# Expert row gathers: GpSimd issues the V row of the running step before the U row of the next step

## The reference, cut to what matters

```
def peer_ffn(x, w_pq, sub_keys1, sub_keys2, peer_u, peer_v):
    q = (xt @ w_pq).reshape(T, PEER_HEADS, PEER_QUERY)
    s1 = einsum(q[..., :128], sub_keys1);  s2 = einsum(q[..., 128:], sub_keys2)
    v1, i1 = top_k(s1, 16);  v2, i2 = top_k(s2, 16)
    top_s, pos = top_k(all 256 sums of v1 and v2, 16)      # 8 heads x 16 = 128 experts for a token
    gate = softmax(top_s)
    u_sel = take(peer_u, idx)                               # rows of 2048 floats
    act = gelu(einsum('thkd,td->thk', u_sel, x), approximate=False) * gate
    v_sel = take(peer_v, idx)
    out = einsum('thk,thkd->td', act, v_sel)
```

## Time and profile before

| | |
|---|---|
| median of 3 runs | 3806.15 us (3805.95 to 3826.44) |
| profiled execution: its time | 3811.37 us |
| profiled execution: span | 3809.3 us |
| PE busy | 3256.0 us (85%) |
| DVE busy | 2196.4 us (58%) |
| POOL busy | 999.7 us (26%) |
| gathers (queue q0) | 547.39 MB, 35.9% of the 16 DMA engines' time |
| weights and gates (queue q1) | 474.45 MB, 32.7% |

### The profile page before, as it was taken

The page is one execution under the profiler, slowest core; times in us unless marked ns, Lnnn a source line. Parts: engine busy times, 40 slices in busy tenths (PEclk is TensorE's granted clock), DMA queues, the critical chain, the costliest instruction groups (busy, mean ns, idle before and its releaser), DMA issues.

```text
span 3809.3 us, 32121 instructions
## 1 busy us (share of the span) xinstructions
PE 3256.0 (85%) x10214; PEld 1893.5 (50%) x10214; DVE 2196.4 (58%) x3100; ACT 378.0 (10%) x653; POOL 999.7 (26%) x674
## 2 busy tenths in 40 slices
PE   7998989899875747377444999999999999999996
PEld 4443433344333323236442666666666666666663
DVE  5455023220168686869996565566656555665654
ACT  1233012210011011101220000000000000000000
POOL 0000000000003222333325443345344334434420
PEclk9999998999987969698776999999999999999998
DMA  6222210012256969697559999999999999999993
GB/s 231 72 77 72 77 61 22 33 66 77 81 188 251 382 230 364 245 375 313 233 227 387 395 379 383 382 403 382 388 393 381 381 381 404 383 387 390 380 362 117
DMA packets 192373, 1022.42 MB, mean 268 GB/s; under 512 B 18368, under 2 KB 51264, under 8 KB 90304
## 3 DMA queue, kind: packets, MB, share of 16 engines
q0 software_dynamic: 75520, 547.39, 35.9%
q1 hardware_dynamic: 116800, 474.45, 32.7%
HBM read 1000.79 MB, written 20.97 MB: 268 GB/s over the span
## 4 chain that ended last, share of the span: by engine, by line
PE 67%; DVE 16%; DMA 10%; issue 5%; ACT 1%; DVEq 0%; SPq 0%; POOL 0%; ACTq 0%; POOLq 0%
PE ps L787 22%; PE ps L801 16%; PE ps L517 9%; DMA arena<-peer_ut 7%; PE ps L656 6%; PE ps L709 3%; DVE arena L1396 2%; DVE arena L1454 2%; PE ps L751 2%; DMA arena<-w_block 1%; DVE arena L1320 1%; DMA arena<-peer_u,arena 1%; PE ps L595 1%; DVE arena L1317 1%; PE ps L611 1%
## 5 line engine op out<-in xcount | busy, mean ns | idle before, releaser
L801 PE MATMUL ps<-arena 128*128 128x512 f32 x2048 | 889.6, 595 | 73.8 <-DVE arena L1467 36.9
L787 PE MATMUL ps<-arena 128*128 128x256 f32 x4096 | 893.9, 378 | 8.4 <-DMA arena<-peer_ut 7.6
L787 PEld LDWEIGHTS ps<-arena 128*128 128x128 f32 x4096 | 767.8, 188 | 144.1 <-DMA arena<-peer_ut 18.6
L437 POOL DMA_INDIRECT arena<-peer_u,arena x256 | 423.3, 1653 | 1225.6 <-DVE arena L1390 1146.7
L801 PEld LDWEIGHTS ps<-arena 128*128 128x128 f32 x2048 | 390.5, 191 | 554.7 <-issue 477.3
L1390 DVE CUSTOM_DVE_ANT_0 arena<-arena 128x2048 f32<-128x2048 f32 x256 | 585.4, 2287 | 90.1 <-DMA arena<-peer_u,arena 87.5
L1396 DVE SCALAR_TENSOR_TENSOR arena<-arena 128x2048 f32<-128x2048 f32 x256 | 601.7, 2350 | 7.8 <-DMA arena<-peer_v,arena 3.3
L437 POOL DMA_INDIRECT arena<-peer_v,arena x256 | 478.2, 1868 | 279.3 <-DVE arena L1396 216.5
L1477 DVE TENSOR_TENSOR arena<-arena,ps 128x512 f32<-128x512 f32 x256 | 162.9, 683 | 469.2 <-PE ps L801 469.1
L517 PE MATMUL ps<-arena 128*128 128x512 f32 x832 | 360.2, 594 | 12.0 <-ACT arena L892 11.0
L709 PE MATMUL ps<-arena 128*128 128x512 f32 x640 | 288.4, 607 | 24.7 <-DMA arena<-w_block 18.8
(11 more groups left out here) (170 smaller groups left out, 1937.1 us busy)
## 6 DMA issues: line engine op xcount, KB each, us to landing
arena<-peer_ut SPq DMA_DIRECT2D x128, 1024.0 KB
arena<-peer_vt SPq DMA_DIRECT2D x128, 1024.0 KB
arena<-w_block SPq DMA_DIRECT2D x192, 512.0 KB
arena<-w_once SPq DMA_DIRECT2D x108, 512.0 KB
dense_gates<-arena SPq DMA_DIRECT2D x8, 2048.0 KB, 6.3
arena<-dense_gates SPq DMA_DIRECT2D x32, 512.0 KB, 24.5
arena<-x SPq DMA_DIRECT2D x4, 1024.0 KB, 21.6
arena<-gains SPq DMA_DIRECT2D x4, 1024.0 KB, 22.7
```

Source lines behind the costliest of these rows:

```text
L437: pool.indirect_dma_start(ring[:, s * D:(s + 1) * D], None, table, bass.IndirectOffsetOnAxis(ap=idx[:, s:s + 1], axis=0)).then_inc(full[s] ...
L787: last = pe.matmul(ps[:, par * 2 + et // 2, (et % 2) * DT:(et % 2 + 1) * DT], w[:, k * P:(k + 1) * P], xt2[:, :, kt, :], start=(kt == 0), ...
L801: last = pe.matmul(bank(4 + (c % 2) * 2 + tb), G[par][:, et * DT + tb * P:et * DT + (tb + 1) * P], w[:, t * 512:(t + 1) * 512], start=(et ...
```

## The change

Inside `rows`, the two calls of `row` in the loop over the four slots change places. The index copies in front of them, the waits themselves, the rings, the last `rows` call with its four V gathers, and the four U gathers issued before the loop stay as they are.

```
                 index(IV[par], j, iv_set, j + 1)
                 for s in range(4):
+                    row(V_RING, peer_v, IV[par], s, v_full, v_free, j * 4 + (s + 1))
                     if not last:
                         row(U_RING, peer_u, IU[1 - par], s, u_full, u_free, j * 4 + (s + 5))
-                    row(V_RING, peer_v, IV[par], s, v_full, v_free, j * 4 + (s + 1))
```

## The result

The changed kernel is slower. Its median is 3843.3 us (3837.39 to 3850.67, 7 runs) against 3811.99 us for the kernel before (3805.95 to 3826.69, 7 runs). The ratio is 1.0078, with a 95% interval of 1.0056 to 1.01, so +30 us (21 to 38). The forecast was +36 us.

A forecast was written before the change was run, and what follows sets the result against it. The prediction took TensorE (busy 995 of 1000 us) to bound the dense part, with the DMA engines almost full. Its terms, 32 + 5 + 2 - 3 = +36 us on 3806.15, gave 3842 us, range 3806 to 3882.

The forecast's parts named there:

- The rule: All steps with a full queue: each U gather lands when the next U gather did before; V gathers get no later.
- Part 1: Dense pairs of steps, VectorE's side: the weigh slips 8.2 us, just using up VectorE's slack; cost 0 to 1 us.
- Rival (b): Dense pairs: VectorE slips 12 us, past its slack, and TensorE waits 4.5 us in each; +75, 3881 us; chance 0.20.
- Part 2: Dense pairs, DMA side: 1.05 MB served later makes gates and weights 2.4 us late in 12 pairs; 32 us in all.
- rival (a): Dense pairs: gates go through in gaps of the gather queue, so the cost is hidden; +4, 3810 us; chance 0.23.
- Part 3: Start of the dense part, four steps in a row: last dot and weigh slip two gathers' time, TensorE waits; 5 us.
- Part 4: Pair of steps at 1792, before the one-hot stage: second and third dot wait for later U gathers; 2 us.
- Part 5: Block-wise part: weights have the DMA engines to themselves while gathers start 4.5 us later; -3 us over three blocks.
- Rival (c): Block-wise part: weights gain while the dense pairs cost nothing; -40 us at most, likely limit -19, 3787 us; chance 0.05.
- rival (d): Opening of each pair: no effect, if the first V slot were free before the first U slot; no chance stated.

The follow-up runs named there:

- e8_only_u0: Kernel before, with the gather order V0 U0 U1 V1 U2 V2 U3 V3, so only the first U gather waits for the first add: 3833.27 us, ratio 1.0058.
- e3_first_u: Kernel before, with the gather order U0 V0 V1 U1 V2 U2 V3 U3, first U gather as before, other three one place later: 3819.75 us, ratio 1.0021.
- e5_gates: Kernel before, with the even groups' gates loaded behind the peer_ut transfers, no gather moved: 3800.97 us, ratio 0.9975.
- e6_gates_v: Changed kernel (V before U everywhere), with the even groups' gates loaded behind the peer_ut transfers: 3811.23 us, ratio 0.9997 against the kernel before.
- e2_dense: Kernel before, with V before U only from rows(20) on, the dense part without its start: 3828.4 us, ratio 1.0045.
- e1_early: Kernel before, with V before U only in rows(0) to rows(13), block-wise part and pair before the one-hot stage: 3817.04 us, ratio 1.0015.
- e4_freeing: Kernel before, with gathers issued in the order VectorE frees the slots, U0 U1 V0 U2 V1 U3 V2 V3: 3794.88 us, ratio 0.9959.

## Why the prediction was right, and where its sizes were off

*The rule* (each U gather lands when the next U gather did before) held to about a us. Before, B's last two stalled dots came 8.4 and 15.9 us after its first one; now the second and third come after 7.6 and 15.0.

*Part 1, VectorE's side of the pairs, 0 to 1 us.* Right. The slip was 6.6 us and not 8.2, inside the slack of 8, and TensorE never waited at line 801 for line 1477 in a pair. The fourth dot came 1.6 us earlier than reckoned. Rival (b), VectorE past its slack, did not come about. GpSimd issued its gathers in 0.94 us during VectorE's stalls, as the forecast had it, but that this kept the slip small was not tried.

*Part 2, the DMA side, 32 us.* The mechanism was right and is shown from three sides. Held back alone, the first U gather brings the waits (e8_only_u0, 22.0 us); left alone in its place, it keeps most of them away (e3_first_u, 10.7 us); and with the gates moved they vanish, stalls or no stalls (e5_gates, e6_gates_v). The term was mis-sized: 16.6 us, half of it. The step that failed is "the 1.05 MB that went through alone at 2355 to 2360 must go through later, within this full stretch", and with it the 2.4 us a pair. About half of these bytes were caught up before the gates' turn came. In the pair shown, 0.95 MB of weights went through while no gather was served; in the next 30 us the weights took 3.87 MB and not 4.71, and the gathers 8.26 MB against 7.82. There 0.61 MB were left, which at 0.383 MB/us are 1.6 us, and from the start of all_v to that of all_u it is 29.50 us against 27.85, 1.65 more. Counted from the packets in the same place of all 14 pairs, 9.4 us after the start of all_v, the gathers are 0.52 MB behind on average, 1.4 us; each pair lost (23.8 - 7.6) / 14 = 1.2 us.

A second step failed too, but it is not what halved the term: "each slot of B is free before its gather's turn comes, so the gather queue has no gap". The gap at 2428 let some 230 packets of gates through beyond one for one, which is rival (a)'s mechanism. But it did not shorten the waits. Take the ten microseconds from 9.3 us after the start of all_v. In eight pairs of the changed kernel the gates got at least 5% more packets there than the gathers, and TensorE waited 2.0 us on average; in the other six it was 1.3. In e8_only_u0 the queues go one for one in all 14 pairs, with 22.0 us of waits. In its first pair (2181 to 2191), where TensorE then waited 2.07 us:

```profile
q0 software_dynamic: 516, 3.81, 92.4%
q1 hardware_dynamic: 519, 0.27, 9.4%
```

The alternation itself is the rule of the Trainium skill, DMA: Bandwidth & Descriptors (section Queues, rings and completion order): each DMA engine takes turns between the queues for which it has work, packet by packet. The trace agrees with it, by 522 packets to 521 in the earlier trace rows; where one queue has a gap, the other gets more, as at 2428 with 318 packets to 89.

*Part 3, the start of the dense part, 5 us.* Measured 5.3. e3_first_u shows that the reason given, two gathers' time in a full queue, is not the whole of it: the same 5.3 us came about with the first U gather in its old place, when U1 was issued 4.5 us later than before. That the number fits is in part luck.

*Part 4, the pair at 1792, 2 us.* The two steps took 36.3 us before (1792.07 to 1828.4) and 40.7 now (1804.90 to 1845.6): 4.4 us, at the upper bound of 4.5. The second dot alone waited 3.25 us. The size is uncertain by some 2 us: the two other kernels with the old order there take 38.1 and 38.3, and the two others with the changed order 41.5 and 40.5.

*Part 5, the block-wise part, -3 us.* Wrong in sign. TensorE's waits for its weights there rose:

```profile
PE ps L709 <- DMA arena<-w_block: 24.4, 15, 1.8
```

They were 18.8. The rise repeats: 18.6 and 19.5 us in the two other kernels with the old order there (e2_dense, e5_gates), 23.8 and 24.0 in the two others with the changed one (e1_early, e6_gates_v). From the first dot to the pair it took 589.9 us against 586.4, +3.5; over the three kernels of each order the means are 593.0 and 586.7, +6, with up to 6 us between the shortest and the longest of one order. The weights did not gain from the later start of the gathers, they lost. In e8_only_u0 the waits are 23.5 us and in e3_first_u 15.6, so it goes with holding back the first U gather; the way from there to the weights was not followed.

*The sum.* 17 + 5 + 4 + 4 = 30 against 32 + 5 + 2 - 3 = 36: the term of part 2 was 15 us too high, and the two small ones 2 and 7 us too low, which hid more than half of that. That the sum came within 6 us is luck to this extent. Rival (c), faster by V first, and rival (d), no effect, are out.

## What to carry to other kernels

When one in-order engine issues the loads of several rings, issue them in the order in which their slots are freed: here that alone was worth 16 us, and each load that was put behind a slot which is freed later gave time away. A transfer that is served while its queue would be empty is free, and the same bytes a few us later are not, even if the engine that uses them has slack; the bill may be paid by another engine, through another queue. Look for what stands at the head of that queue: half a MB in packets of 512 bytes, ahead of weights that TensorE needed next, was what turned late bytes into a wait, and behind them it cost the dense part nothing.

## What the runs showed of the hardware that I had not expected

- GpSimd gets faster where VectorE stalls, as forecast, and the effect is large: with 84 us more stalls in the dense part, GpSimd's busy time over the span fell from 999.7 to 863.3 us, and in e4_freeing, with almost no stalls, it was 1051.5. In the dense part a gather's issue took 0.93 to 0.96 us where VectorE was idle all the while, and mostly 1.9 to 3.0 us beside a dot or an add.
- Executions differ by some 16 us before the point where the kernels begin to differ (first dot at 1199.2 to 1215.0 us in ten profiles), so two profiles can only be compared stretch by stretch. Where TensorE never waits, the dense part repeats to 0.1 us (1683.7, 1683.8 and 1683.7); with the same order of gathers and waits in it, it repeated to 0.3 us (1694.7 and 1695.0).
- A wait of 1.9 to 2.7 us in a stretch in which TensorE is otherwise always busy was followed in five places by 3.4 us of the granted clock at half, which cost 1.7 us each.
